# Stick-breaking attention: one round trip per head, or three sweeps over pairs of heads

## What is computed

```python
for blk in range(L // SB_BLOCK):
    ...
    z = jnp.einsum("bhtd,bhsd->bhts", q[:, :, q0:lk], k[:, :, :lk]).astype(jnp.float32) * scale
    ...
    mask = s_idx < t_idx
    log_keep = jnp.where(mask, jax.nn.log_sigmoid(-z), 0.0)
    log_remain = lax.cumsum(log_keep, axis=3, reverse=True) - log_keep
    log_a = jnp.where(mask, jax.nn.log_sigmoid(z) + log_remain, -jnp.inf)
    a = jnp.exp(log_a)
    outs.append(jnp.einsum("bhts,bhsd->bhtd", a.astype(v.dtype), v[:, :, :lk]))
...
o_a = rms_norm(o_a.transpose(0, 2, 1, 3).reshape(B_, L, GROUP_W), sb_norm_g[l])
```

## Time and profile before

| | |
|---|---|
| median of 3 runs | 3598.17 us (3593.76 to 3600.09) |
| profiled execution | 3598.53 us, of which the span of its instructions 3596.8 us |
| PE busy in the span | 2991.2 us (83%) |
| DVE, ACT, POOL busy | 1412.0, 843.5, 120.0 us |
| TensorE clock granted, mean | 0.895 of full speed (1.0 is 2.4 GHz, 0.5 is 1.2 GHz) |
| the stretch of stick_breaking and its norm | 1740 to 1872 us |

### The profile page before, as it was taken

One profiled execution on the slowest core, in us unless ns is written; L12 is line 12 of the kernel. 1 busy time (PEld: TensorE's weight loads), 2 busy tenths in 40 slices (PEclk: granted clock), 3 DMA queues, 4 the chain that ended last, 5 costly groups with the idle time before them and its releaser, 6 DMA issues. The chain is left out here.

```text
span 3596.8 us, 34659 instructions
## 1 busy us (share of the span) xinstructions
PE 2991.2 (83%) x12934; PEld 1989.5 (55%) x12935; DVE 1412.0 (39%) x2488; ACT 843.5 (23%) x1336; POOL 120.0 (3%) x132
## 2 busy tenths in 40 slices
PE   6887779998967899999644365899999999999983
PEld 5656658887745688878421245444454444444431
DVE  3863464444365544443346742542121121111113
ACT  4343343223123422231452121100000000000001
POOL 0520000000000000000002000000000000000001
PEclk9997889999978999999656667799999999999986
DMA  3201214443212132212100004499998899998994
GB/s 113 70 24 47 82 65 164 166 177 128 94 48 81 48 110 101 94 59 95 46 2 1 1 0 152 156 380 386 388 332 309 316 379 337 364 333 315 378 349 170
DMA packets 289248, 616.98 MB, mean 172 GB/s; under 512 B 9539, under 2 KB 15330, under 8 KB 288962
## 3 DMA queue, kind: packets, MB, share of 16 engines
q1 hardware_dynamic: 274432, 564.50, 43.6%
q10 hardware_dynamic: 12322, 41.38, 2.9%
q0 software_dynamic: 2304, 8.39, 0.6%
HBM read 575.18 MB, written 39.06 MB: 171 GB/s over the span
## 5 line engine op out<-in xcount | busy, mean ns | idle before, releaser
L2703 PE MATMUL psum<-expert_ring,hT 128*128 128x512 f32 x832 | 373.9, 603 | 26.1 <-issue 26.1
L87 DVE TENSOR_TENSOR unit_low<-unit_whole,unit_high 128x4096 fp32r<-128x4096 f32 (+3 forms) x65 | 283.2, 4358 | 194.4 <-ACT unit_high L84 194.2
L84 ACT ACTIVATE unit_high<-unit_whole 128x4096 fp32r<-128x4096 f32 (+3 forms) x65 | 225.6, 3471 | 501.3 <-PE psum L643 275.1
L2717 PE MATMUL psum<-expert_ring,hT 128*64 128x512 f32 x1344 | 301.6, 602 | 18.3 <-DMA expert_ring<-in_moe_w_gu 11.9
L2703 PEld LDWEIGHTS psum<-expert_ring,hT 128*128 128x128 f32 x832 | 160.1, 193 | 228.4 <-issue 227.4
L2717 PEld LDWEIGHTS psum<-expert_ring,hT 128*64 128x64 f32 x1344 | 101.5, 139 | 207.8 <-issue 205.9
L643 PE MATMUL psum<-high_parts,unit_high 128*128 128x512 f32 x512 | 200.9, 392 | 6.0 <-DVE low_parts L87 6.0
L643 PE MATMUL psum<-low_parts,unit_high 128*128 128x512 f32 x512 | 200.7, 392 | 0.0
L643 PE MATMUL psum<-high_parts,unit_low 128*128 128x512 f32 x512 | 200.5, 392 | 0.0
L643 PE MATMUL psum<-unit_high,hidden_high 128*128 128x512 f32 x512 | 199.6, 390 | 0.0
L643 PE MATMUL psum<-unit_high,hidden_low 128*128 128x512 f32 x512 | 199.3, 389 | 0.0
(11 more groups left out here) (588 smaller groups left out, 4863.7 us busy)
## 6 DMA issues: line engine op xcount, KB each, us to landing
expert_ring<-in_moe_w_gu SPq DMA_DIRECT2D x136, 2048.0 KB, 15.1
expert_ring<-in_moe_w_down SPq DMA_DIRECT2D x68, 2048.0 KB, 13.5
unit_whole<-in_w_up SPq DMA_DIRECT2D x16, 2048.0 KB, 8.8
unit_whole<-in_w_down SPq DMA_DIRECT2D x16, 2048.0 KB, 7.7
expert_rows<-zero_row ACTq DMA_DIRECT2D x15, 1536.0 KB, 5.3
unit_whole<-in_w_in SPq DMA_DIRECT2D x5, 2048.0 KB, 7.8
unit_whole<-in_w_in_e SPq DMA_DIRECT2D x4, 2048.0 KB, 7.9
unit_whole<-in_wkv_x SPq DMA_DIRECT2D x4, 2048.0 KB, 8.0
```

The costliest lines, as they stand in the source:

```text
L84: return act.activation(self.high, self.whole, ACT.Copy)
L87: return dve.tensor_tensor(self.low, self.whole, self.high.bitcast(F32), ALU.subtract)
L2703: pe.matmul(bank, xg[:, c, :], w[:, c, :], start=(c == 0), stop=False)
L2717: pe.matmul(banks[g], xg[:, c, 0:HALF], w[g][:, c, :], start=(c == 0), stop=False)
```

## The change

`stick_breaking` is written anew. A unit is now two heads and one tile (`StickUnit`), eight units, the longest first. All scores come first: PE runs through the eight units with four pairs of banks, DVE copies the masked scores to SBUF (`z`; for the four long units in `hT`, which is free there, for the others in `stick_scores`), and ACT takes Abs of unit u and Exp of unit u - 1 in turn. Then ACT takes Ln of all units. Then, unit by unit, DVE adds max(z, 0), and scans the sum backwards over the keys with a row of zeros as the second operand; POOL subtracts it from z; ACT takes Exp without bias; PE turns both heads, DVE copies the first out and ACT the second, into the place of the weights; PE multiplies by the values and ACT saves both heads at once. The norm and the turn with the gain follow in the same block. The mask and the identity of the score product are bf16, and the factor 1/8 is put on the queries when the projection is copied out.

```diff
@@ -1843,78 +1843,201 @@
-def stick_breaking(k, units, scale):
...
+class StickUnit:
+    def __init__(self, group, t, qT, kT, v):
+        self.group, self.t, self.keys = group, t, (t + 1) * P
+        self.q = [qT[64 * c:64 * c + 64, group, t * P:self.keys] for c in range(2)]
+        self.k = [kT[64 * c:64 * c + 64, group, 0:self.keys] for c in range(2)]
+        self.v = [[v[:, m, (2 * group + c) * 64:(2 * group + c + 1) * 64] for m in range(t + 1)] for c in range(2)]
+def stick_breaking(k, qT, kT, v, o, late, gain, dst):
+    SCORES, TURNED, OUT = 4, 4, 6
+    units = [StickUnit(g, t, qT, kT, v) for t in range(TT - 1, -1, -1) for g in range(2)]
...
+        early = k.sb("stick_scores", [P, 3 * 4 * P], ctx=ctx)
+        soft = k.sb("stick_soft", [P, 10 * 4 * P], ctx=ctx)
+        zeros = k.sb("stick_zeros", [P, S], ctx=ctx)
...
+        before = [2 * sum(un.keys for un in units[:u]) for u in range(n)]
+        z = [pair(late, before[u], u) if units[u].t >= 2 else pair(early, before[u] - before[4], u) for u in range(n)]
+        s = [pair(soft[:, :], before[u], u) for u in range(n)]
...
+                pe.wait_ge(masks, 1)
+                for u, un in enumerate(units):
+                    if u >= SCORES:
+                        pe.wait_ge(copied, u - SCORES + 1)
+                    for c in range(2):
+                        pe.matmul(score_banks(u)[:, c, :], un.q[c], un.k[c], start=True, stop=False)
+                    for c in range(2):
+                        ins = pe.matmul(score_banks(u)[:, c, un.t * P:], ident[:, :], strict[:, :], start=False, stop=True)
+                    ins.then_inc(scored, 1)
+                def turn_probs(u):
+                    pe.wait_ge(probs_ready, u + 1)
+                    for c in range(2):
+                        if u >= 1:
+                            pe.wait_ge(first_copied if c == 0 else second_copied, u)
+                        else:
+                            pe.wait_ge(copied, n)
+                        for m in range(units[u].t + 1):
+                            ins = pe.transpose(turned_bank(u, c)[:, m * P:(m + 1) * P], s[u][:, c, m * P:(m + 1) * P],
+                                               k.ident[:, :])
+                        ins.then_inc(turned, 1)
+                def values(u):
+                    un = units[u]
+                    if u >= 2:
+                        pe.wait_ge(out_saved, u - 1)
+                    for c in range(2):
+                        pe.wait_ge(first_copied if c == 0 else second_copied, u + 1)
+                        for m in range(un.t + 1):
+                            ins = pe.matmul(out_bank(u)[:, 64 * c:64 * c + 64], s[u][:, c, m * P:(m + 1) * P], un.v[c][m],
+                                            start=(m == 0), stop=(m == un.t))
+                    ins.then_inc(out_ready, 1)
+                for u in range(n):
+                    turn_probs(u)
+                    if u >= 1:
+                        values(u - 1)
+                values(n - 1)
...
+                pe.wait_ge(k.normalised.sem, k.normalised.at(1))
+                for c in range(2):
+                    for t in range(TT):
+                        ins = pe.transpose(k.psum[:, c, t * P:(t + 1) * P], o[:, t, c * P:(c + 1) * P], k.ident[:, :])
+                    ins.then_inc(k.turned.sem, 1)
...
                 for u in range(n):
+                    act.wait_ge(copied, u + 1)
+                    act.activation(s[u], z[u], ACT.Abs).then_inc(decayed, 1)
+                    if u >= 1:
+                        act.wait_ge(decayed, u)
+                        act.activation(s[u - 1], s[u - 1], ACT.Exp, scale=-1.0).then_inc(powers, 1)
+                act.wait_ge(decayed, n)
+                act.activation(s[n - 1], s[n - 1], ACT.Exp, scale=-1.0).then_inc(powers, 1)
+                for u in range(n):
+                    act.wait_ge(powers, u + 1)
+                    act.activation(s[u], s[u], ACT.Ln, bias=1.0).then_inc(logs, 1)
+                def probabilities(u):
+                    act.wait_ge(logged, u + 1)
+                    act.activation(s[u], z[u], ACT.Exp).then_inc(probs_ready, 1)
+                def save(u):
+                    act.wait_ge(out_ready, u + 1)
+                    un = units[u]
+                    act.activation(o[:, un.t, un.group * P:(un.group + 1) * P], out_bank(u), ACT.Copy).then_inc(out_saved, 1)
+                def square(t):
+                    u = 2 * (TT - 1 - t) + 1
+                    act.wait_ge(out_saved, u + 1)
+                    act.activation(early[:, t * 256:(t + 1) * 256], o[:, t, :], ACT.Square, accum_out=ss[:, t:t + 1]).then_inc(squared, 1)
+                probabilities(0)
+                probabilities(1)
+                for u in range(n):
+                    act.wait_ge(turned, 2 * u + 2)
+                    act.activation(s[u][:, 1, :], turned_bank(u, 1), ACT.Copy).then_inc(second_copied, 1)
                     if u + 2 < n:
+                        probabilities(u + 2)
+                    if u >= 1:
+                        save(u - 1)
+                save(n - 1)
+                for t in range(TT - 1, -1, -1):
+                    square(t)
+                act.wait_ge(squared, TT)
+                act.activation(rms[:, :], ss[:, :], ACT.Sqrt, bias=k.eps[:, 0:1], scale=1.0 / 256)\
+                   .then_inc(k.roots.sem, 1)
+                act.wait_ge(k.turned.sem, k.turned.at(2))
+                act.activation(dst[:, 1, :], k.psum[:, 1, :], ACT.Copy, scale=gain[:, 1:2]).then_inc(k.turned_odd.sem, 1)
...
+                for u in range(n):
+                    pool.wait_ge(summed, u + 1)
+                    pool.tensor_tensor(z[u], z[u], s[u], ALU.subtract).then_inc(logged, 1)
...
+                k.dve.step(dve, dve.memset(zeros[:, :], 0.0))
+                dve.tensor_copy(strict[:, :], k.strict[:, :])
+                dve.tensor_copy(ident[:, :], k.ident[:, :]).then_inc(masks, 1)
                 for u in range(n):
+                    dve.wait_ge(scored, u + 1)
+                    dve.tensor_copy(z[u], score_banks(u)).then_inc(copied, 1)
+                def sums(u):
+                    dve.wait_ge(logs, u + 1)
+                    k.dve.step(dve, dve.scalar_tensor_tensor(out=s[u], in0=z[u], scalar=0.0, in1=s[u], op0=ALU.max,
+                                                             op1=ALU.add))
+                    for c in range(2):
+                        ins = dve.tensor_tensor_scan(s[u][:, c, ::-1], s[u][:, c, ::-1], zeros[:, 0:units[u].keys], 0.0,
+                                                     ALU.add, ALU.add)
+                    ins.then_inc(summed, 1)
+                def copy(u):
+                    dve.wait_ge(turned, 2 * u + 1)
+                    dve.tensor_copy(s[u][:, 0, :], turned_bank(u, 0)).then_inc(first_copied, 1)
+                sums(0)
+                sums(1)
+                for u in range(n):
                     if u + 2 < n:
+                        sums(u + 2)
+                    copy(u)
+                dve.wait_ge(k.roots.sem, k.roots.at(1))
+                k.dve.step(dve, dve.reciprocal(rstd[:, :], rms[:, :]))
+                dve.tensor_tensor(o, o, rstd[:, :].unsqueeze(2).broadcast_to([P, TT, 256]), ALU.mult)\
+                   .then_inc(k.normalised.sem, 1)
+                dve.wait_ge(k.turned.sem, k.turned.at(1))
+                dve.tensor_scalar(dst[:, 0, :], k.psum[:, 0, :], gain[:, 0:1], None, ALU.mult)\
+                   .then_inc(k.turned_even.sem, 1)
...
@@ -2530,24 +2653,19 @@
-        project(k, [{"unit": u + j, "banks": b} for j, b in enumerate(banks)],
-                lambda dve, j, b, bank: dve.tensor_copy(homes[j][b], bank), [tokens])
+        def save(dve, j, b, bank):
+            if j == 0 and b < 2:
+                return dve.tensor_scalar(homes[j][b], bank, 64 ** -0.5, None, ALU.mult)
+            return dve.tensor_copy(homes[j][b], bank)
+        project(k, [{"unit": u + j, "banks": b} for j, b in enumerate(banks)], save, [tokens])
...
         projection.close()
         mixT = k.hT
-        stick_breaking(k, [{"q": [half(h, 0, slice(t * P, (t + 1) * P))], "k": [half(h, 2, slice(0, (t + 1) * P))],
-                            "keys": (t + 1) * P, "mask": (k.ident[:, :], k.strict[:, :], t * P),
-                            "v": [sb_v[:, m, h // 2 * P:(h // 2 + 1) * P] for m in range(t + 1)],
-                            "first": 64 * (h % 2),
-                            "out": sb_o[:, t, h * 64:(h + 1) * 64]} for h in range(4) for t in range(TT)],
-                       64 ** -0.5)
+        stick_breaking(k, sb_qk[:, 0:2, :], sb_qk[:, 2:4, :], sb_v, sb_o[:, :, :],
+                       mixT[:, :, :].rearrange("p c s -> p (c s)"), k.col("sb_norm_g_2", 0, 2), mixT[:, 0:2, :])
         inner.close()
-        heads_norm(k, [(by_head(sb_o[:, :, :], 256), by_head(sb_o[:, :, :], 256), None)])
```

(8 more changed lines are left out.)

75 lines of the change are left out of this document (22 added, 53 removed).

## The result

| | before | after |
|---|---|---|
| median of 4 runs each | 3597.22 us (3593.76 to 3600.09) | 3512.71 us (3508.47 to 3518.59) |
| profiled execution, of which span | 3598.5, 3596.8 us | 3518.6, 3516.8 us |
| ACT busy in the span | 843.5 us | 801.4 us |
| stage, its first instruction to the next stage's | 132.0 us | 63.9 us |

The changed kernel takes 0.9767 of the time before, 95% interval 0.9747 to 0.9787: **84.5 us** less. The prediction said 3532 with a range of 3519 to 3546; the measured time lies 6 us under the range. The stage itself came out nearly as forecast: 63.9 us, where 66.0 was put. So 68.1 us were gained there (66.0 forecast), and some 16 us were gained where nothing was forecast. Medians of one kernel differ by up to 3.5 us between sets of runs (the kernel before: 3597.2 to 3600.7), so small gains are read from places in the traces.

The account below looks back on a forecast made before the run. No engine was the bound: the stage was a round trip between ACT and PE. The new steps summed to 64.9 us, 65.9 with the clock, taken as 66.0 against 132.0; 3598.5 - 66 = 3532.5, as a median 3532, range 3519 to 3546.

Parts of the forecast that it names:

- the last sentence of its first part: Around the stage: everything stands in blocks before and after, so the end should lose what the stage loses, 66.0 us.
- nothing is added to any DMA queue: Whole kernel: listed among the things that cost nothing; no DMA queue gets more work.
- rival (5): Behind the stage: the gain does not reach the end because something later waits for an unmoved moment; chance 0.01.
- Tables: ACT in the stage: loads fall from 34 to 4 with the norm's root, 38.5 us off ACT.
- First sweep: Stage start: ACT paces Abs and Exp over eight units, with scores and copies hidden under them; 17.6 us.
- the 1.0 us for it: First sweep: allowance for PE's clock falling; 1.2 GHz all through would add 2.5 us to the scores.
- Third sweep: Sums, subtractions, last Exp, turns and values: DVE's 20.6 and POOL's 12.1 us in turns, from 20.0 to 53.9.
- backward scans at the forward price: DVE in the third sweep: 16 backward scans cost what forward ones do, 13.2 us, 1.23 us at 512.
- Turns of POOL and DVE: Third sweep: POOL and DVE take turns, scans included, at 20.6 + 12.1 us and eight hand-overs of 0.15.
- The clock: PE in the third sweep: its clock rises from 0.50 to 1.00 behind units 0 and 1, so PE keeps up.
- rival (2): Third sweep: PE stays at 1.2 GHz, waiting for probabilities in every unit; stage 70 to 71 us, time 3537; chance 0.12.
- End: Last save to next stage: squares, root, product, transposes, copy; 8.6 us, nearly at par with the norm and turn blocks before.

Follow-up runs that it names:

- after_pad108: The changed kernel with 108 instructions of long-past waits on PE between the last scores and the first turn; 3527.41 us (ratio 0.9798).
- after_pad36: The changed kernel with 36 instructions of long-past waits on PE between the last scores and the first turn; 3528.22 us (ratio 0.9809).
- after_lnper: The changed kernel with each unit's logarithm directly behind its exponential, not in a sweep of its own; 3521.69 us (ratio 0.9784).

## Why the prediction was wrong, point by point

- **The step that failed** is the last sentence of its first part: everything around the stage stands in blocks, so the end loses what the stage loses. The blocks do stand, but their code does not: a change of PE's program moves all that follows against the packets in which it is fetched, and three jumps far behind the stage went from 26.1 to 10.9 us, the loop around them from 1254.3 to 1240.9. The prediction had this at nothing: "nothing is added to any DMA queue" looked at data and not at instructions, and rival (5) asked only whether a gain could be lost on the way, and looked only at moments of time. With the loop moved back to where its jumps cost 26.2 us (`after_pad108`) or 21.7 (`after_pad36`), the changed kernel takes 3527.4 and 3528.2 us, inside the range and 4 to 5 us from the forecast. Of the rest of the miss, 2.1 us are the stage's.
- **Tables:** right, 34 to 4 loads. That their time would be gained was never a term, and `after_lnper` shows why that was well: 18 us of loads put back cost 7 to 9.
- **First sweep:** 17.6 forecast, 15.5 measured. One pass of ACT over all units is shorter (eight logarithms in 5.12 us where a pass was put at 5.9), because records in a row overlap by some 0.1 us, and PE's clock was 1.00, so the 1.0 us for it was not needed. DVE's sums started at 17.9, not 20.0.
- **Third sweep:** backward scans at the forward price, right. Turns of POOL and DVE, right, and the scans are in: 4.36 us against 2.34. The Trainium skill ("SBUF — State Buffer", Who interferes with whom) states it for a DVE instruction with two SBUF inputs against a GpSimd one that reads SBUF; the trace agrees. The sum was too strict: 30.9 us from the first sum to the last subtraction, where 33.9 were put.
- **The clock:** wrong. It was to rise behind units 0 and 1, by what a stretch of other work did, and stayed at 0.50 through 23 us without a pause. The third sweep ended at 56.1 us, as forecast (56.3), by luck: this error and the two before it cancel, for the sums were done 5 us early and PE was 5 us late. That is rival (2)'s mechanism, priced 6 to 7 us too high (70 to 71 for the stage), since the sums that it starts from were early.
- **End:** 8.6 forecast, 7.8 measured (four squares 1.7 and not 2.5, the records overlapping again). "Nearly at par" was right.

## What to carry to other kernels

A gain in one stage can be joined or eaten by a loop far behind it: where the idle time ahead of a branch says "issue" and the instruction queue shows a packet in the gap, shift the loop by harmless instructions in several steps (22 changed nothing here, 36 and 108 did) before reading anything else into it, and compare two versions at the same place. Where an engine is waiting anyway, count what a wait is under before calling it free. And when a new stage runs PE behind another engine, look at the granted clock first: here 64 products that nobody reads took 10 us off the stage.

## What the runs showed of the hardware that was not expected

- The same jump cost 3.6, 5.1, 7.1 (in two parts) or 8.7 us, by the place of the code alone: 15 us of idle time in a kernel with three such jumps.
- PE's clock did not rise in 23 us of turns and values of 64 columns without a pause at 0.50, rose behind 16 turns of 128 columns in 3.7 us, and once up held at 1.00 through the same turns and values. What decides it is left open; no run varied it by itself.
- Waits that are long past are not free: the records of 234 such instructions in a row stand 106 ns apart, 25 us in all, of which 22 lay on PE's path.
- Another instruction queue, q14, carried 71 packets in the changed kernel and 48 before; the changed kernel has some in every round of the experts' loop, the kernel before has none from 2514 to 3352 us. No wait was seen that they end.
